# Low halves of the layer weights: from GpSimd to VectorE in the mixing part of a layer

## The chip, the cores and the metric

The kernel runs on one core of one Trainium2 chip. The metric is the device time of one execution in microseconds (us); less is better. TensorE (PE), VectorE (DVE), ScalarE (ACT), GpSimd (POOL) and SyncE (SP, which issues the DMAs) each run their own list of instructions in order and meet through semaphores.

## The reference

A first block (attention, pooling, a mixture of experts, a gated projection) is followed by two equal layers of a second block. Only these two layers are touched. Cut to what is computed:

```python
for l in range(2):
    x = x + 0.5 * swiglu(rms_norm(x, ffa_norm[l]), ffa_w_in[l], ffa_w_out[l])      # feed-forward, part 1
    h = rms_norm(x, mix_norm[l])
    (c_q, c_kv, k_rope, g_q, g_k, g_v, g_b, g_a, g_z, m_qkv, gate_logits) = split_cols(h @ w_in[l], IN_SPLITS)
    o_mla = mla_branch(...)      # latent attention: up-projection, norm of each head, RoPE, causal attention
    o_gdn = gdn_branch(...)      # convolution, l2 norm, gated delta rule in chunks
    o_moba = moba_branch(...)    # norm of each head, RoPE, causal attention
    up = einsum('bsnw,nwd->bsnd', stack([o_mla, o_gdn, o_moba], axis=2), w_branch[l])
    x = x + sum(sigmoid(gates) * up, axis=2) @ w_out[l]
    x = x + 0.5 * swiglu(rms_norm(x, ffb_norm[l]), ffb_w_in[l], ffb_w_out[l])      # feed-forward, part 2
```

256 rows, width 1024, everything in float32.

## The kernel before, in words

**Split weights.** A float32 product is made of three faster ones (`mm3`, L502): each operand is held as a high part in the type fp32r and a low part, which is the rest. Activations are split where they are made. Weights come from memory in float32 and are split on the chip. They stream in steps (`STEPS`, L36), each of two halves of 2048 words a partition (`HALVES`), each half of two pieces of 1024 words (some smaller). A piece passes four engines:

- SP loads it into one of four buffers `raw` (L1676), once the piece that lay there four pieces ago has its low part (semaphore `weights_split`).
- ACT writes the high part into `w_hi` (`hi_act`, L483), one of three slots of a half each. Before the first piece of a half it waits until PE has used the half that lay in the slot, three halves back (`half_read`).
- POOL subtracts and writes the low part into `w_lo` (`lo_pool`, L489).
- PE waits for the low part of a half and multiplies (`weights`, L493, and L504 to L506).

ACT's copies stand between its other work, where `Splits.ahead(step)` (L430) is called: it puts out all pieces of the halves up to three beyond the last of the step named. POOL has nothing else to do in a layer.

**Order in a layer.** Feed-forward part 1, the mixing part (`MIX_STEPS`, L33), feed-forward part 2. In the mixing part PE runs: `mla` (the latents), gates 0, up-projection, gates 1 and 2, latent attention; `moba` 0 to 2, gates 3 and 4, branch 0, the second attention; `gdn` 0 to 2, `z`, gates 5, the delta rule (`gdn_pe`, L749), branches 2 and 1, output projection. VectorE works on what PE needs next: the head norms (L644 to L650) and RoPE (L662 to L667), on which the transposes of an attention (L309) wait; the convolution (L913, L915) and the l2 norm (L926 to L934), on which the delta rule waits; the sum of the branches (L1838 to L1847), on which the output projection waits. PSUM has eight banks, and PE claims a bank only when its reader has freed it (`claim`).

Of the diff's functions `gdn_dve` (from L885) and the blocks of `layer_body` (from L1668) hold most of the places that the texts name.

Of the kernel before, what the change touches and what calls it, by code (L numbers as in the profile page):

```python
# [423 lines left out]
class Splits:  # L424
# [5 lines left out]
    def ahead(self, step):  # L430

        upto = min(last_half_of(step) + SPLIT_SLOTS + 1, len(HALVES))
# [52 lines left out]

def lo_pool(k, pool, i):
    for n, at in pieces(i):
        pool.wait_ge(k.sem("weights_hi"), n + 1)
        k.nc.gpsimd.tensor_tensor(k.w[1][i % SPLIT_SLOTS][:, at], k.raw[n % RAW_SLOTS][:, 0:at.stop - at.start],  # L489
                                  k.w[0][i % SPLIT_SLOTS][:, at], ALU.subtract).then_inc(k.sem("weights_split"), 1)  # L490


def weights(k, pe, step, shape):  # L493

    own = [i for i, h in enumerate(HALVES) if h[0] == STEP[step]]
    for h, i in enumerate(own):
        pe.wait_ge(k.sem("weights_split"), 2 * i + 2)
        words = HALVES[i][2]
        yield h, h == len(own) - 1, [k.w[j][i % SPLIT_SLOTS][:, 0:words].rearrange("p (c n) -> p c n", n=shape) for j in range(2)]
# [47 lines left out]
def norm2_dve(k, dve, link, n, gain, power):  # L547
    nc, st = k.nc, k.s(STATS, SCRATCH - STATS)
    V_ = nc.vector
    dve.wait_ge(k.sem("ss_ready"), 2 * (n + 1))  # L550
    rstd_dve(k, dve, link, st[:, 0:2], 1.0 / D, power)
    for t in range(NT):
        V_.tensor_scalar(k.h[:, t, :], k.x[:, t, :], st[:, t:t + 1], None, ALU.mult).then_inc(k.sem("h_ready"), 1)
    for half in range(2):
# [63 lines left out]
def ffn_dve(k, dve, n):  # L618
    nc = k.nc
    silu, prod = k.s(SILU_TMP, 2, 512), k.s(SILU_TMP + 1024, 2, 512)  # L620
    for kind, u in FFN_STEPS:
        if kind == "out":
            continue
        b, free = k.filled(dve, ("up", n, u))
# [260 lines left out]
def gdn_dve(k, dve, link):  # L885
# [21 lines left out]
    for i in range(3):  # L907
        k.evacuated(dve, ("raw", i, 0), ("raw", i, 1))
        for j in range(4):
# [35 lines left out]
    link(V_.tensor_copy(G.XT[:, :].rearrange("p t h n -> p (t h) n"), bc(k.c("ident").unsqueeze(1), [P, 8, P])))  # L945
    branch_dve(k, dve, 2)
# [710 lines left out]
def layer_body(k, dram, layer):  # L1657
# [9 lines left out]
    with nc.Block() as block:  # L1667
        @block.sync  # L1668
        def _(sp):
            sp.dma_start(k.lvec[:, :], dram["lvec"][bass.ds(layer, 1)].rearrange("o p n -> (o p) n")).then_inc(k.sem("lvec_loaded"), 16)  # L1670
            for i, (step, at, _words) in enumerate(HALVES):
                for n, part_at in pieces(i):
                    if n >= RAW_SLOTS:
                        sp.wait_ge(k.sem("weights_split"), n - RAW_SLOTS + 1)
# [117 lines left out]
        def _(dve):  # L1792
# [3 lines left out]
            norm2_dve(k, dve, link, 0, k.lv("g_ffa"), 0)  # L1796
            ffn_dve(k, dve, 0)
            norm2_dve(k, dve, link, 1, k.lv("g_mix"), 1)
            k.evacuated(dve, ("mla", 0), ("mla", 1))
# [10 lines left out]
            ins.then_inc(k.sem("c_ready"), 1)  # L1810
            gain = k.lv("c_norm")
# [12 lines left out]
            dve.wait_ge(k.sem("k_rope"), 2)  # L1824
            k.evacuated(dve, *[(x, t, i) for t in range(NT) for x in ("q", "kv") for i in range(2)])
            head_norm_dve(k, dve, link, mla.qk, k.s(QKT, 32, MLA_D), MLA_D, (k.lv("q_norm"), k.lv("k_norm")), 3)
            rope_dve(k, dve, link, mla.qk, QKT, 64, 16, k.c("cos16"), k.c("sin16"), k.sem("qk_ready"))
            mask = lambda t, pair: bc(causal[:, (1 - t) * P:2 * P].unsqueeze(1), [P, 2, (t + 1) * P])
            attn_dve(k, dve, link, mla, MLA_D ** -0.5, mask)
            k.evacuated(dve, *[("moba", i, t) for i in range(3) for t in range(NT)])  # L1830
            head_norm_dve(k, dve, link, moba.qk, k.s(QKT, 32, MOBA_D), MOBA_D, (k.lv("moba_q"), k.lv("moba_k")), 4)
            rope_dve(k, dve, link, moba.qk, QKT, 0, 32, k.c("cos32"), k.c("sin32"), k.sem("qk_ready"))
            branch_dve(k, dve, 0)
            attn_dve(k, dve, link, moba, MOBA_D ** -0.5, mask)
            gdn_dve(k, dve, link)

            branches = gatesT.rearrange("p (n c) s -> p n c s", n=3)
            link(V_.tensor_tensor(comb, branches[:, 0], branches[:, 2], ALU.add))  # L1838
            branch_dve(k, dve, 1)
# [8 lines left out]
            for v in range(2):  # L1848
                for t in range(NT):
# [4 lines left out]
            ffn_dve(k, dve, 1)  # L1854
# [178 lines left out]
```

## Time and profile before

| | us |
|---|---|
| Median of 3 runs (2852.99 to 2853.11) | 2853.03 |
| Span of the profiled execution, first to last instruction | 2852.2 |
| Layer 0: first matmul of the layer to that of layer 1 | 1172.65 to 2016.25, 843.6 |
| of it the mixing part, about | 436 |
| PE busy over the span | 2534.9 (89%) |
| DVE, ACT, POOL busy | 973.9, 888.3, 1027.5 |

The profile gives the profiled execution's span; what lies around it is the difference to the median, 0.8 us. A busy PE is not at its peak: its clock has two levels, 2.4 GHz (granted clock 1.0) and 1.2 GHz (0.5). Layer 1 repeats layer 0 to within 0.5 us, so the texts speak of layer 0 and count twice. Times in the rows are us from the start of the span.

### The profile page before, as it was taken

To read this page: it belongs to the slowest core of one execution; us is meant where nothing else is said; L and a number is where in the kernel's file an instruction comes from. 1 tells how busy PE (TensorE), PEld (TensorE's weight loads), DVE (VectorE), ACT (ScalarE), POOL (GpSimd) and SP (SyncE) were. 2 spreads that over 40 slices of the span, in tenths; PEclk is the share of its full clock that TensorE was granted. 3 is DMA by queue.
4 is the path that set the end of the run, shared out by engine and by line. 5 is a ranking of instruction groups with operands and counts; after the bars stand their busy time and mean duration, and the time that the engine had idled before them with its cause. 6 is when DMAs were issued, how large, how long until landed. Compare 5 with 4: busy or idle time off the path is not lost. (4 is left out here: it accounts for less than half of the span.)

```text
span 2852.2 us, 37927 instructions
## 1 busy us (share of the span) xinstructions
PE 2534.9 (89%) x15142; PEld 1826.0 (64%) x15142; DVE 973.9 (34%) x1514; ACT 888.3 (31%) x1266; POOL 1027.5 (36%) x428
## 2 busy tenths in 40 slices
PE   8889999999999998799778976899799777986899
PEld 3544443434434343599767866899799767875898
DVE  0322121212222121311465775221211557774221
ACT  1311212111111211444344531343444444431342
POOL 0000000000000000488548521688688546522686
PEclk9889999999999999899889997999899888997999
DMA  8249999999999995455325320354455324311453
GB/s 333 97 180 428 429 428 428 429 428 429 427 430 427 430 428 243 134 185 185 133 68 170 103 75 30 132 185 157 161 186 185 123 86 136 119 60 40 153 187 138
DMA packets 94236, 650.66 MB, mean 228 GB/s; under 512 B 10448, under 2 KB 12416, under 8 KB 68128
## 3 DMA queue, kind: packets, MB, share of 16 engines
q1 hardware_dynamic: 94112, 648.94, 58.8%
q8 instruction: 86, 1.41, 0.2%
q14 instruction: 38, 0.31, 0.0%
HBM read 647.84 MB, written 1.06 MB: 228 GB/s over the span
## 5 line engine op out<-in xcount | busy, mean ns | idle before, releaser
L489 POOL TENSOR_TENSOR w_lo<-raw,w_hi 128x1024 fp32r<-128x1024 f32 (+3 forms) x424 | 1027.3, 2446 | 1807.5 <-ACT w_hi L483 1807.5
L1319 PE MATMUL bank<-ring,scratch 128*64 128x512 f32 x3072 | 686.1, 596 | 27.2 <-DMA ring<-in_expert_units 25.4
L483 ACT CAST w_hi<-raw 128x1024 fp32r<-128x1024 f32 (+3 forms) x424 | 419.8, 1038 | 672.0 <-PE bank L506 659.6
L504 PE MATMUL bank<-hT_hi,w_hi 128*128 128x256 f32 x1984 | 566.1, 285 | 18.6 <-ACT scratch L1762 9.5
L505 PE MATMUL bank<-hT_lo,w_hi 128*128 128x256 f32 x1984 | 565.0, 285 | 0.0
L506 PE MATMUL bank<-hT_hi,w_lo 128*128 128x256 f32 x1984 | 564.9, 285 | 0.0
L1319 PEld LDWEIGHTS bank<-ring,scratch 128*64 128x64 f32 x3072 | 209.7, 137 | 455.0 <-issue 386.7
L504 PEld LDWEIGHTS bank<-hT_hi,w_hi 128*128 128x128 f32 x1984 | 384.8, 194 | 21.6 <-issue 10.5
L505 PEld LDWEIGHTS bank<-hT_lo,w_hi 128*128 128x128 f32 x1984 | 384.8, 194 | 0.8
L506 PEld LDWEIGHTS bank<-hT_hi,w_lo 128*128 128x128 f32 x1984 | 384.5, 194 | 0.0
L1487 DVE TENSOR_TENSOR scratch<-bank,scratch 128x512 f32<-128x512 f32 x64 | 44.3, 692 | 605.0 <-PE bank L1333 601.1
L626 DVE TENSOR_TENSOR scratch<-scratch,bank 128x512 f32<-128x512 f32 x44 | 30.3, 688 | 539.2 <-ACT scratch L612 539.2
L504 PE MATMUL bank<-w_hi,act_hi 128*128 128x512 f32 (+1 forms) x376 | 147.2, 392 | 6.9 <-ACT scratch L1027 6.9
L505 PE MATMUL bank<-w_lo,act_hi 128*128 128x512 f32 (+1 forms) x376 | 147.1, 391 | 0.0
L506 PE MATMUL bank<-w_hi,act_lo 128*128 128x512 f32 (+1 forms) x376 | 146.7, 390 | 0.0
L1305 PEld LDWEIGHTS bank<-scratch,h_rows 128*128 128x128 f32 x1056 | 124.9, 194 | 27.5 <-issue 27.5
L1305 PE MATMUL bank<-scratch,h_rows 128*128 128x128 f32 x1056 | 133.8, 281 | 0.0
L745 PE MATMUL bank<-scratch 128*128 128x128 f32 x816 | 106.0, 293 | 26.2 <-DVE scratch L986 7.3
L745 PEld LDWEIGHTS bank<-scratch 128*128 128x128 f32 x816 | 102.4, 206 | 32.0 <-issue 18.0
L1388 ACT COPY scratch<-bank 128x512 f32<-128x512 f32 x64 | 37.5, 586 | 265.9 <-PE bank L1319 265.9
L1390 ACT ACTIVATE scratch<-scratch 128x256 f32<-128x256 f32 x64 | 26.7, 417 | 276.2 <-DVE scratch L1490 276.2
L629 DVE TENSOR_TENSOR act_lo<-scratch,act_hi 128x512 fp32r<-128x512 f32 x44 | 102.3, 2324 | 30.2 <-ACT act_hi L615 30.2
(263 smaller groups left out, 2832.8 us busy)
## 6 DMA issues: line engine op xcount, KB each, us to landing
ring<-in_expert_units SPq DMA_DIRECT2D x192, 2048.0 KB, 20.5
raw<-in_layer_units SPq DMA_DIRECT2D x408, 512.0 KB, 4.7
ring<-in_first_units SPq DMA_DIRECT2D x6, 2048.0 KB, 23.9
ring<-in_ple_units SPq DMA_DIRECT2D x2, 2048.0 KB, 9.9
raw<-in_layer_units SPq DMA_DIRECT2D x8, 424.0 KB, 3.4
raw<-in_layer_units SPq DMA_DIRECT2D x4, 384.0 KB, 3.2
const<-in_const SPq DMA_DIRECT2D x1, 1184.0 KB, 7.3
x_res<-in_x SPq DMA_DIRECT2D x1, 1024.0 KB, 4.9
```

The source lines that it names most:

```text
L483: k.nc.scalar.copy(k.w[0][i % SPLIT_SLOTS][:, at], k.raw[n % RAW_SLOTS][:, 0:at.stop - at.start]).then_inc(k.sem("weights_hi"), 1)
L489: k.nc.gpsimd.tensor_tensor(k.w[1][i % SPLIT_SLOTS][:, at], k.raw[n % RAW_SLOTS][:, 0:at.stop - at.start], k.w[0][i % SPLIT_SLOTS][:, at], ...
L504: nc.tensor.matmul(out, lhsT[0], rhs[0], start=start, stop=False)
L505: nc.tensor.matmul(out, lhsT[0], rhs[1], start=False, stop=False)
L506: return nc.tensor.matmul(out, lhsT[1], rhs[0], start=False, stop=stop)
L626: nc.vector.tensor_tensor(prod[:, u % 2, :], silu[:, u % 2, :], b[:, :], ALU.mult).then_inc(free, 1)
L629: nc.vector.tensor_tensor(lo, prod[:, u % 2, :], hi, ALU.subtract).then_inc(k.sem("act_lo"), 1)
L745: last = nc.tensor.matmul(b[:, h * P:(h + 1) * P], lhsT[:, h, :], rhs[:, h, :], start=True, stop=True)
L1305: last = nc.tensor.matmul(b[:, j * P:(j + 1) * P], k.h[:, t, c * P:(c + 1) * P], sel[:, t, :], start=(t == 0), stop=(t == 1))
L1319: last = nc.tensor.matmul(b[g * SL:(g + 1) * SL, :], lhsT[:, c, :], w[:, c, g, :], start=start and c == 0, stop=stop and c == 3)
L1388: nc.scalar.copy(rows[:, half, :], b[:, :]).then_inc(free, 1)
L1487: V_.tensor_tensor(both, b[:, :].rearrange("p (a n) -> p a n", n=SL), bc(wide_bias, [P, 8, SL]), ALU.add)\
```

## The change

The low parts of the 80 pieces of the mixing part are now computed by VectorE (`lo_dve`), those of the feed-forward parts still by GpSimd (132 pieces a layer). The semaphore `weights_split` is replaced by two, and `split_done` says for a piece which one and which count. In `gdn_dve` and in VectorE's block of `layer_body` calls of `splits.ahead` (and of the new `to`) are put between its other work, at about the places where ScalarE has them. ScalarE's and TensorE's instructions keep their order.

```diff
+FIRST_MIX = sum(1 for h in HALVES if STEPS[h[0]][0] == "ffn0")
+LAST_MIX = sum(1 for h in HALVES if STEPS[h[0]][0] != "ffn1")
+def split_done(k, n):
+    i = n // 2
+    if FIRST_MIX <= i < LAST_MIX:
+        return k.sem("mix_weights_split"), n - 2 * FIRST_MIX + 1
+    return k.sem("ffn_weights_split"), n + 1 if i < FIRST_MIX else n + 1 - 2 * (LAST_MIX - FIRST_MIX)
...
+def lo_dve(k, dve, i):
+    if not FIRST_MIX <= i < LAST_MIX:
+        return
+    for n, at in pieces(i):
+        dve.wait_ge(k.sem("weights_hi"), n + 1)
+        k.nc.vector.tensor_tensor(k.w[1][i % SPLIT_SLOTS][:, at], k.raw[n % RAW_SLOTS][:, 0:at.stop - at.start],
+                                  k.w[0][i % SPLIT_SLOTS][:, at], ALU.subtract).then_inc(k.sem("mix_weights_split"), 1)
...
-        pe.wait_ge(k.sem("weights_split"), 2 * i + 2)
+        pe.wait_ge(*split_done(k, 2 * i + 1))
...
-                        sp.wait_ge(k.sem("weights_split"), n - RAW_SLOTS + 1)
+                        sp.wait_ge(*split_done(k, n - RAW_SLOTS))
...
+            splits.ahead(STEP["gates", 0])
             gain = k.lv("c_norm")
...
+            splits.ahead(STEP["up_proj", 0])
             k.evacuated(dve, *[(x, t, i) for t in range(NT) for x in ("q", "kv") for i in range(2)])
             head_norm_dve(k, dve, link, mla.qk, k.s(QKT, 32, MLA_D), MLA_D, (k.lv("q_norm"), k.lv("k_norm")), 3)
+            splits.ahead(STEP["gates", 1])
             rope_dve(k, dve, link, mla.qk, QKT, 64, 16, k.c("cos16"), k.c("sin16"), k.sem("qk_ready"))
...
+            splits.ahead(STEP["gates", 2])
             attn_dve(k, dve, link, mla, MLA_D ** -0.5, mask)
+            for i in range(3):
+                splits.ahead(STEP["moba", i])
             k.evacuated(dve, *[("moba", i, t) for i in range(3) for t in range(NT)])
             head_norm_dve(k, dve, link, moba.qk, k.s(QKT, 32, MOBA_D), MOBA_D, (k.lv("moba_q"), k.lv("moba_k")), 4)
+            splits.ahead(STEP["gates", 3])
             rope_dve(k, dve, link, moba.qk, QKT, 0, 32, k.c("cos32"), k.c("sin32"), k.sem("qk_ready"))
+            splits.ahead(STEP["gates", 4])
+            splits.ahead(STEP["branch", 0])
             branch_dve(k, dve, 0)
...
             branches = gatesT.rearrange("p (n c) s -> p n c s", n=3)
             link(V_.tensor_tensor(comb, branches[:, 0], branches[:, 2], ALU.add))
+            splits.ahead(STEP["branch", 1])
             branch_dve(k, dve, 1)
...
         def _(pool):
             for i in range(len(HALVES)):
-                lo_pool(k, pool, i)
+                if not FIRST_MIX <= i < LAST_MIX:
+                    lo_pool(k, pool, i)
```

VectorE, head norm and RoPE of the latent attention, before (L647 and L650 end the norm, L662 to L667 are RoPE, whose first half is shown):

```order
L647 TENSOR_TENSOR scratch<-scratch 128x3072
L650 TENSOR_TENSOR scratch<-scratch,lvec 128x1536 x2
L662 TENSOR_TENSOR scratch<-scratch,const 128x256
L663 TENSOR_TENSOR scratch<-scratch,const 128x256
L664 TENSOR_TENSOR scratch<-scratch,const 128x256
```

And after the change (the lines have moved: L676, L679 and L691 are L647, L650 and L662 of before; L514 is the new subtraction):

```order
L676 TENSOR_TENSOR scratch<-scratch 128x3072
L679 TENSOR_TENSOR scratch<-scratch,lvec 128x1536 x2
L514 TENSOR_TENSOR w_lo<-raw,w_hi 128x1024 x4
L691 TENSOR_TENSOR scratch<-scratch,const 128x256
L692 TENSOR_TENSOR scratch<-scratch,const 128x256
L693 TENSOR_TENSOR scratch<-scratch,const 128x256
```

Four pieces stand between the norm and RoPE now; in the second attention four stand at the same place.

VectorE, end of the convolution and l2 norm of the delta rule, before (L915 convolution, L923 squares, L926 to L934 l2 norm):

```order
L915 SCALAR_TENSOR_TENSOR scratch<-scratch,lvec 128x256 x12
L923 TENSOR_TENSOR scratch<-scratch 128x1024 x2
L926 TENSOR_SCALAR scratch<-bank 128x512 x4
L930 RECIPROCAL scratch<-scratch 128x512 x4
L933 SCALAR_TENSOR_TENSOR scratch<-scratch 128x1024
```

And after the change:

```order
L945 SCALAR_TENSOR_TENSOR scratch<-scratch,lvec 128x256 x12
L514 TENSOR_TENSOR w_lo<-raw,w_hi 128x1024 x4
L954 TENSOR_TENSOR scratch<-scratch 128x1024 x2
L957 TENSOR_SCALAR scratch<-bank 128x512 x4
L514 TENSOR_TENSOR w_lo<-raw,w_hi 128x1024 x4
L962 RECIPROCAL scratch<-scratch 128x512 x4
L965 SCALAR_TENSOR_TENSOR scratch<-scratch 128x1024
```

Four pieces stand ahead of the squares and four ahead of the reciprocals.

## Rows read from the trace of the kernel before

**Rows 1.** The page: the span.

```profile
span 2852.2 us, 37927 instructions
```

**Rows 2.** Windows: feed-forward 1, mixing; us, busy PE, PEld, DVE, ACT, POOL, PEclk, DMA share, GB/s.

```profile
1172.00:1367.00 195.00, 191.07 (x1335) 180.54 (x1336) 42.80 (x47) 82.88 (x93) 165.04 (x70) 0.98 0.56 187
1367.00:1803.00 436.00, 342.72 (x2269) 312.15 (x2268) 265.85 (x324) 168.56 (x271) 200.06 (x81) 0.87 0.29 95
```

**Rows 3.** Waits of PE, both layers: waiting line, releaser, total us, times, longest.

```profile
PE bank L309 <- DVE scratch L667: 52.8, 4, 14.1
PE bank L504 <- DVE hT_lo L1847: 17.6, 2, 8.8
PE bank L755 <- DVE scratch L923: 10.8, 2, 5.4
```

**Rows 4.** The page's groups: busy us, mean ns; idle before, releaser.

```profile
L489 POOL TENSOR_TENSOR w_lo<-raw,w_hi 128x1024 fp32r<-128x1024 f32 (+3 forms) x424 | 1027.3, 2446 | 1807.5 <-ACT w_hi L483 1807.5
L483 ACT CAST w_hi<-raw 128x1024 fp32r<-128x1024 f32 (+3 forms) x424 | 419.8, 1038 | 672.0 <-PE bank L506 659.6
```

**Rows 5.** Groups of DVE by form.

```profile
L629 DVE TENSOR_TENSOR act_lo<-scratch,act_hi 128x512 fp32r<-128x512 f32 x44 | 102.3, 2324 | 30.2 <-ACT act_hi L615 30.2
...
L626 DVE TENSOR_TENSOR scratch<-scratch,bank 128x512 f32<-128x512 f32 x44 | 30.3, 688 | 539.2 <-ACT scratch L612 539.2
...
L923 DVE TENSOR_TENSOR scratch<-scratch 128x1024 f32<-128x1024 f32 x4 | 4.7, 1220 | 0.0
```

**Rows 6.** Timeline of DVE, norm to RoPE: start, duration, operation, [idle before].

```profile
1371.66 1.68 DVE L205 TENSOR_SCALAR scratch<-scratch 128x2 f32<-128x2 f32 x1 [3.42 <-ACT h_rows L233]
...
1402.80 0.56 DVE L1815 TENSOR_TENSOR act_hi<-bank,lvec 128x384 fp32r<-128x384 f32 x1 [3.46 <-PE bank L1695]
...
1426.27 3.35 DVE L645 TENSOR_REDUCE scratch<-scratch 128x32 f32<-128x3072 f32 x1
...
1437.42 5.53 DVE L647 TENSOR_TENSOR scratch<-scratch 128x3072 f32<-128x3072 f32 x1 [5.37 <-ACT scratch L212]
1442.99 7.66 DVE L650 TENSOR_TENSOR scratch<-scratch,lvec 128x1536 f32<-128x1536 f32 x2
...
1458.91 0.42 DVE L667 TENSOR_TENSOR scratch<-scratch 128x256 f32<-128x256 f32 x1
```

**Rows 7.** Timeline of ACT around gates 0 and gates 2.

```profile
1402.47 1.99 ACT L483 CAST w_hi<-raw 128x1024 fp32r<-128x1024 f32 x2 [4.19 <-PE bank L506]
...
1447.27 1.08 ACT L1027 ACTIVATE scratch<-bank 128x512 f32<-128x512 f32 x2
```

**Rows 8.** Timeline of PE: both attentions, l2 norm, after branch 2.

```profile
1459.39 0.88 PE L309 MATMUL bank<-const,scratch 128*96 128x128 f32 x3 [14.06 <-DVE scratch L667]
...
1564.64 5.33 PE L309 MATMUL bank<-const,scratch 128*64 128x128 f32 x32 [12.36 <-DVE scratch L667]
...
1658.64 1.55 PE L755 MATMUL bank<-scratch,const 128*128 128x512 f32 x3 [1.79 <-ACT scratch L1027]
...
1682.87 1.16 PE L780 MATMUL bank<-const,scratch 128*128 128x128 f32 x8 [1.67 <-DVE scratch L1612]
```

**Rows 9.** Windows after a wait of PE (4.75 us before 1420.03); columns as in rows 2.

```profile
1420.00:1424.40 4.40, 4.37 (x20) 4.40 (x21) 3.24 (x1) 1.03 (x4) 3.01 (x2) 0.50 0.62 212
1424.70:1445.30 20.60, 20.60 (x172) 20.43 (x171) 15.09 (x6) 9.75 (x11) 14.01 (x6) 1.00 0.38 124
```

**Rows 10.** Timeline of DVE, second attention: end of the norm, RoPE.

```profile
1532.86 4.47 DVE L647 TENSOR_TENSOR scratch<-scratch 128x2048 f32<-128x2048 f32 x1 [4.33 <-ACT scratch L212]
1537.37 6.67 DVE L650 TENSOR_TENSOR scratch<-scratch,lvec 128x1024 f32<-128x1024 f32 x2
1544.07 2.78 DVE L662 TENSOR_TENSOR scratch<-scratch,const 128x512 f32<-128x512 f32 x1
```

**Rows 11.** Timeline of DVE, delta rule: reciprocals of the l2 norm.

```profile
1661.27 12.98 DVE L930 RECIPROCAL scratch<-scratch 128x512 f32<-128x512 f32 x4
```

**Rows 12.** Timeline of ACT, after the convolution: high parts behind L859.

```profile
1652.81 3.87 ACT L483 CAST w_hi<-raw 128x1024 fp32r<-128x1024 f32 x4
```

More of the change, by code:

```diff
@@ L430, in ahead, with to @@
     def ahead(self, step):
-        upto = min(last_half_of(step) + SPLIT_SLOTS + 1, len(HALVES))
+        self.to(last_half_of(step) + SPLIT_SLOTS + 1)
+    def to(self, end):
+        upto = min(end, len(HALVES))
         for i in range(self.done, upto):
@@ L489, in lo_pool @@
         k.nc.gpsimd.tensor_tensor(k.w[1][i % SPLIT_SLOTS][:, at], k.raw[n % RAW_SLOTS][:, 0:at.stop - at.start],
-                                  k.w[0][i % SPLIT_SLOTS][:, at], ALU.subtract).then_inc(k.sem("weights_split"), 1)
+                                  k.w[0][i % SPLIT_SLOTS][:, at], ALU.subtract).then_inc(k.sem("ffn_weights_split"), 1)
+def lo_dve(k, dve, i):
[5 more added lines that the diff above has]
+                                  k.w[0][i % SPLIT_SLOTS][:, at], ALU.subtract).then_inc(k.sem("mix_weights_split"), 1)
 def weights(k, pe, step, shape):
@@ L542, in rows3_pe, with norm2_dve @@
             last.then_inc(k.sem("half_used"), 1)
-def norm2_dve(k, dve, link, n, gain, power):
+def norm2_dve(k, dve, link, n, gain, power, between=lambda: None):
     nc, st = k.nc, k.s(STATS, SCRATCH - STATS)
@@ L553, in norm2_dve @@
         V_.tensor_scalar(k.h[:, t, :], k.x[:, t, :], st[:, t:t + 1], None, ALU.mult).then_inc(k.sem("h_ready"), 1)
+    between()
     for half in range(2):
@@ L615, in ffn_act, with ffn_dve @@
         k.nc.scalar.copy(k.act2[0][:, at:at + 2, :].rearrange("p c n -> p (c n)"), prod[:, u % 2, :]).then_inc(k.sem("act_hi"), 1)
-def ffn_dve(k, dve, n):
+def ffn_dve(k, dve, n, splits):
     nc = k.nc
@@ L622, in ffn_dve @@
         if kind == "out":
+            if u < FFN_OUT_UNITS - 1:
+                splits.ahead(STEP[f"ffn{n}", kind, u])
             continue
+        splits.ahead(STEP[f"ffn{n}", kind, u])
         b, free = k.filled(dve, ("up", n, u))
@@ L882, in gdn_act, with gdn_dve @@
         nc.scalar.copy(k.act2[0][:, 4:8, t * P:(t + 1) * P], part(b, 4, P)).then_inc(k.sem("go_hi"), 1)
-def gdn_dve(k, dve, link):
+def gdn_dve(k, dve, link, splits):
     nc, G = k.nc, Gdn(k)
@@ L907, in gdn_dve @@
     for i in range(3):
+        splits.ahead(STEP["gdn", i])
         k.evacuated(dve, ("raw", i, 0), ("raw", i, 1))
@@ L919, in gdn_dve @@
                 ins.then_inc(k.sem("conv_ready"), 1)
+    splits.ahead(STEP["z", 0])
     for i in range(2):
@@ L926, in gdn_dve @@
         V_.tensor_scalar(G.sq[:, 2 * b4:2 * b4 + 2, :], part(b, 2, S), EPS, None, ALU.add).then_inc(free, 1)
+    splits.ahead(STEP["gates", 5])
     for b4 in range(4):
@@ L945, in gdn_dve @@
     link(V_.tensor_copy(G.XT[:, :].rearrange("p t h n -> p (t h) n"), bc(k.c("ident").unsqueeze(1), [P, 8, P])))
+    splits.ahead(STEP["branch", 2])
     branch_dve(k, dve, 2)
@@ L1795, in _ @@
             dve.wait_ge(k.sem("lvec_loaded"), 16)
-            norm2_dve(k, dve, link, 0, k.lv("g_ffa"), 0)
-            ffn_dve(k, dve, 0)
+            splits = Splits(k, dve, lo_dve)
+            norm2_dve(k, dve, link, 0, k.lv("g_ffa"), 0, lambda: splits.to(1))
+            splits.to(SPLIT_SLOTS)
+            ffn_dve(k, dve, 0, splits)
             norm2_dve(k, dve, link, 1, k.lv("g_mix"), 1)
+            splits.ahead(STEP["ffn0", "out", 5])
+            splits.ahead(STEP["mla", 0])
             k.evacuated(dve, ("mla", 0), ("mla", 1))
@@ L1848, in _ @@
             for v in range(2):
+                if v == 0:
+                    splits.ahead(STEP["wout", v])
                 for t in range(NT):
@@ L1853, in _ @@
             norm2_dve(k, dve, link, 2, k.lv("g_ffb"), 6)
-            ffn_dve(k, dve, 1)
+            splits.ahead(STEP["wout", 1])
+            ffn_dve(k, dve, 1, splits)
         @block.gpsimd
```

2 lines of the change are left out of this document (1 added, 1 removed).

## The prediction

> **What bounds the kernel now.** I read the windows first, then PE's waits, then the timelines of VectorE, ScalarE and PE around the longest waits. In the feed-forward window PE is busy 191 of 195 us; in the mixing window 343 of 436 [rows 2]. What can be won lies in the mixing window. PE's waits name no POOL instruction: the low part is never late. A piece costs POOL 2.45 us [rows 4], so a half 4.9, while PE needs 5.76 for one (48 matmuls at 20.60/172 = 0.12 us [rows 9]). PE waits for VectorE: 52.8 us for the end of RoPE, 17.6 for the sum of the branches, 10.8 for the end of the convolution [rows 3].
>
> POOL does matter in another way. VectorE's L626 (one input in PSUM) takes 0.69 us, and L629, as long but with both inputs in SBUF, 2.32 [rows 5]. In the second attention the 512-long L662 takes 2.78, against the 0.69 of L626 [rows 5, 10]: it waits some 2.1 us, most of one POOL instruction. The 1024-long L650 takes 3.33 each, against 1.22 for L923 [rows 5, 10]. So VectorE and POOL block each other when both read SBUF, and just in the head norms, on which PE waits.
>
> The Trainium skill has this in "SBUF — State Buffer", Who interferes with whom: VectorE with two SBUF inputs and GpSimd take turns at a shared port, and the loser waits for the whole instruction. By the rows the wait is about 2.1 of 2.45 us. By the whole-instruction rule each blocked VectorE instruction would gain some 0.3 us more than I count, about 2 us a layer; I go by the rows.
>
> **The change, step by step, for layer 0, in the clock of before.** It moves 80 pieces a layer to VectorE. Durations: 1.22 us (L923 [rows 5]) for 1024 long; lengths 3072 and 1536 without POOL are 3.35 (L645 [rows 6]) and, between 1.22 and 3.35, 1.75; a short RoPE instruction 0.38 from start to start (0.42 with overlap [rows 6]), a long one 0.61 to 0.69. 80 x 1.22 = 98 us on an engine busy 266 of 436 [rows 2]: it does not become the bound by its sum. The question is what each group of pieces stands in front of, and when PE gets its halves: it holds at most three that are ready.
>
> 1. *Norm before mixing.* L205 takes 1.68 us for two elements [rows 6], a wait for POOL. VectorE makes the last pieces before it. Bounds 0 to -1.68; I take -1.5.
> 2. *Up-projection.* VectorE starts L1815 at 1402.80. Now the last two pieces of `ahead(gates 0)` stand ahead, whose high parts ACT writes from 1402.47 to 1404.46 [rows 6, 7]: second low part at 1405.7, and L1815 is 2.9 late, of which 0.7 was cover, since PE waits for ACT's sigmoid too. +2.2. Position +0.7.
> 3. *First attention.* PE waited 14.06 us until 1459.39 [rows 8], so gates 2 ended at 1445.3 and the half before it at 1439.6. After the change PE stops at 1440.3, since the last half of gates 2 is split only behind L650. L647 starts when ACT has the root (1437.42 [rows 6]) + 0.7, then 3.35 + 2 x 1.75: 1445.0. Two pieces: 1447.4. PE stops 7.1 us, then 5.76: 1453.2. It needs a bank that ACT frees: 2.6 us, as before (L1027 at 1447.27 [rows 7] + 0.6, against 1445.3): 1455.8. RoPE is ready earlier (1445.0 + 4 x 1.2 + 12 x 0.38 = 1454.4). L309 starts at 1455.8 for 1459.39: position -3.6, term -4.3.
> 4. *Second attention.* The same. PE's wait was 12.36 until 1564.64 [rows 8], so its halves ended at 1535.0, 1540.8, 1546.5, 1552.3. It stops at 1535.0; L650 ends at 1532.86 + 2.3 + 2.4 = 1537.6 (2.3: two of 1.22, less one fixed cost), and two pieces later, 1540.0, it goes on: a stop of 5. Three halves: 1557.3; the last is split behind RoPE (1542.4 + 12 x 0.61 + 2.4 = 1552.1), some 0.8 late: 1558.1, for 1564.64, -6.5. But banks 4 to 7 are freed by L1612, now behind eight pieces, whose high parts follow PE's last halves: I take +2.4 (bounds 0 and 8 x 1.22 = 9.8). Term -4.1.
> 5. *Convolution.* Without POOL its 48 instructions end before PE is through with gates 5, with 12 pieces among them. PE's wait of 5.4 (half of 10.8 [rows 3]) goes. The third L755 waits for ACT's sigmoid at 1658.64 [rows 8], behind L483 that started only at 1652.81 [rows 12], when the convolution was done; this moves forward by as much as PE allows. I take -4.6 (bounds 0 and -5.4).
> 6. *l2 norm.* Four pieces stand ahead of the reciprocals (12.98 us, no wait ahead [rows 11]), on which the delta rule waits. 4 x 1.15: +4.6, no cover.
> 7. *Branch 2.* Four more ahead of L1612, on which L780 waits [rows 8]: +4.8, of which up to 1.7 is PE's slack there; +3.1.
> 8. *Output projection.* Four pieces ahead of branch 1's evacuation, mostly under PE's matmuls. +1.0 (bounds 0 and 4.9).
>
> Sum: -1.5 + 2.2 - 4.3 - 4.1 - 4.6 + 4.6 + 3.1 + 1.0 = -3.6 a layer. The feed-forward parts are unchanged.
>
> 9. *TensorE's clock.* After a wait of 4.75 us PE did 20 matmuls in 4.4 us at granted clock 0.50 (1.2 GHz), where 2.4 GHz does 20 x 0.12 = 2.4 [rows 9]: a stop costs 2.0 more. Before, the two long waits were followed by transposes; now two new stops are followed by dense matmuls. Bounds 0 and +4.0 a layer, and below nothing too, since elsewhere waits vanish; I take one, +2.2.
>
> Net -1.4 a layer, -2.8 for two. The profiled execution spans 2852.2, 0.8 below the median [rows 1]: 2852.2 - 2.8 + 0.8 = **2850.2 us**.
>
> "TensorE: Matmul & The Clock Gate", HAM oscillation, in the Trainium skill says that a matmul stream cut up by waits is throttled again at each, which speaks against this change. By it both stops cost, and the sum is near nothing; a result of its own only with more stops, below.
>
> **Rivals.** 0.2% is 5.7 us, about what a measurement of this kernel tells from no change.
>
> *Forecast: losses and gains cancel* (chance 0.40). Within 2847 to 2859. For it: two groups of terms of about 13 us each a layer, on the same engine.
>
> *The port pays more* (0.35), 2840 to 2847. The steps won are full, and the pieces of steps 6 to 8 find cover: if 7 and 8 cost half and the clock nothing, it is -3.6 - 2.0 = -5.6 a layer, 2842. For it: the gains are read from rows, PE's wait of 12.36 us [rows 8] could be nearly all won. Against: step 6 stands bare.
>
> *Slower, by the clock* (0.25), 2859 to 2870. The two long waits become many short ones, PE runs at 1.2 GHz behind each. It decides from the third stop on that is followed by dense matmuls: with both stops of steps 3 and 4, one more in the moba and branch halves and one at branch 1, 4 x 2.0 = 8 for the 2.2 that I took: -3.6 + 8 = +4.4 a layer, 2862. For it: granted clock 0.87 in the mixing window with ten waits over 2 us. Against: the long waits' own restart goes.
>
> *VectorE's waits for high parts hold back the critical work*, part of that chance: a subtraction waits for ACT, ACT for PE, and what is queued behind it on VectorE waits with it. The worst place is before L1612 (step 4); at its bound of 9.8 it gives +7.4 a layer more, 2865.
>
> *It doesn't do what it says* (below 0.02): POOL would still run in the mixing part.
>
> Range for 8 of 10: 2839 to 2864. Faster by over 0.2% 0.35, within 0.40, slower 0.25.
>
> **What would show it.** POOL idle in the mixing window, VectorE near 266 + 98 - 50 = 314 busy. Right: L650's counterpart at 1.22 and 1.75; PE waits before a half of gates 2 (some 7 us) and of gates 4 (some 5), both with the new subtraction as releaser; PE's wait for RoPE gone or under 3; the wait before L755 gone; the delta rule's start 7 to 8 us later against the end of gates 5. Wrong: long waits of PE for RoPE that stay (then the port was not the cause), stops for low parts elsewhere, or a granted clock in the mixing window under 0.85.

## The result, and the profile after

The changed kernel takes 2866.44 us (four executions, 2859.28 to 2872.11), the kernel before 2853.07 beside it: ratio 1.0044, 95% interval 1.0029 to 1.0058. It is slower by 13 us; 2850.2 were predicted, in a range up to 2864. Fifteen executions in three sets have the median 2868.7; two lie at 2859, the rest between 2865 and 2872. The first profiled one, from which the rows here are, is the fastest of them (2859.28). One execution of one experiment (`after_between`) took 6918.6 us where its five others took 2832 to 2842, and is left out of its ratio.

Its windows for the feed-forward and the mixing part of layer 0, with the columns of [rows 2]:

```profile
1171.60:1367.00 195.40, 191.12 (x1329) 180.66 (x1330) 45.61 (x49) 83.64 (x95) 157.19 (x66) 0.97 0.58 188
1367.00:1810.00 443.00, 355.07 (x2277) 322.52 (x2275) 280.04 (x403) 171.35 (x273) 10.11 (x5) 0.87 0.30 95
```

GpSimd has gone from the mixing part: its 10 us in this window are pieces of the feed-forward part. VectorE is busy 280 us of it; the pieces in the window cost 88, and 74 of that came back from its other instructions (265.9 + 87.8 - 280.0). The prediction had 50 coming back and 314 busy. The 1024-long subtraction, by VectorE's groups by form:

```profile
L514 DVE TENSOR_TENSOR w_lo<-raw,w_hi 128x1024 fp32r<-128x1024 f32 x144 | 169.3, 1221 | 126.8 <-ACT w_hi L487 126.4
```

TensorE's waits over both layers (waiting line, releaser, total, times, longest), to be held against [rows 3]:

```profile
PE bank L529 <- DVE w_lo L514: 24.7, 4, 7.2
...
PE bank L529 <- DVE hT_lo L1894: 19.2, 2, 9.6
...
PE bank L809 <- DVE scratch L1645: 12.6, 2, 6.4
...
PE bank L774 <- DVE scratch L966: 11.0, 2, 5.6
...
PE bank L309 <- DVE scratch L1645: 6.4, 2, 3.7
PE bank L309 <- ACT scratch L1060: 6.4, 2, 3.4
```

The 52.8 us for the end of RoPE and the 10.8 for the end of the convolution are gone. In their place stand stops for a low part (7.24 and 5.11 us in each layer), and for what VectorE does behind its pieces: L809 behind the evacuation of branch 2 (L1645), L774 behind the l2 norm (L966), the transposes L309. The wait for the sum of the branches stays and grows (19.2 for 17.6).

VectorE in the first attention, where [rows 6] are its rows of before (start, duration, operation, idle before):

```profile
1428.71 0.18 DVE L205 TENSOR_SCALAR scratch<-scratch 128x32 f32<-128x32 f32 x1
...
1437.60 3.36 DVE L676 TENSOR_TENSOR scratch<-scratch 128x3072 f32<-128x3072 f32 x1 [8.32 <-ACT scratch L212]
1440.99 3.56 DVE L679 TENSOR_TENSOR scratch<-scratch,lvec 128x1536 f32<-128x1536 f32 x2
1444.58 4.63 DVE L514 TENSOR_TENSOR w_lo<-raw,w_hi 128x1024 fp32r<-128x1024 f32 x4
1449.13 0.42 DVE L691 TENSOR_TENSOR scratch<-scratch,const 128x256 f32<-128x256 f32 x1
```

The norm's product takes 3.36 us for 5.53, the two gain products 3.56 for 7.66. But ScalarE's root comes 3 us later after its reciprocal than before (8.32 us of idle for 5.37), and four pieces of 1.15 stand ahead of RoPE.

Cut at TensorE's first instruction of each stage, a layer divides as follows. "Before" is the mean of its two layers, "after" the mean over three profiled executions (`after`, `after_again` and `after_third`: 2859, 2870 and 2866 us), all in us; the second layer's last feed-forward part is taken to TensorE's last instruction; "port free" and "pieces short" are two experiments told below.

| stretch, by TensorE | before | after | predicted change | measured | port free | pieces short |
|---|---|---|---|---|---|---|
| norm before mixing to the first attention | 83.8 | 84.7 | -2.1 | +0.9 | 72.9 | 79.8 |
| to the second attention | 105.3 | 99.5 | -6.5 | -5.8 | 93.4 | 98.3 |
| second attention | 25.6 | 28.1 | +2.4 | +2.5 | 24.6 | 25.1 |
| convolution, to the end of the l2 sums | 70.2 | 64.1 | -4.6 | -6.1 | 64.4 | 63.9 |
| l2 norm, to the KK products | 17.3 | 21.9 | +4.6 | +4.6 | 17.4 | 17.7 |
| to the transposes of v (branch 2) | 5.1 | 10.0 | +3.1 | +4.9 | 5.1 | 8.4 |
| delta rule | 71.2 | 72.1 | 0 | +0.9 | 71.7 | 71.3 |
| branch 1, output projection | 56.7 | 58.9 | +1.0 | +2.2 | 53.0 | 56.7 |
| both feed-forward parts | 401.1 | 401.8 | -1.5 | +0.7 | 400.6 | 401.1 |

Step 1 of the prediction (-1.5) shortens TensorE's wait ahead of the norm's first product, so it lies in the last row, and steps 2 and 3 make the -2.1 of the first. Predicted -3.6, and +2.2 for the clock: -1.4. Measured +4.7 in this mean of profiles, 9.4 for two layers. The three spans are 10.9 us longer than before; the other 1.5 lie ahead of layer 0, where no instruction was changed.

### The profile page after: what moved, and what is told of

Its sections match the earlier page's. It is cut to its first block and busy times, and to the rows that moved or that the text cites. A ratio compares the mean times of both kernels' runs of the same rounds, so it can differ in the third digit from the quotient of the medians.

```text
span 2857.4 us, 37933 instructions
## 1 busy us (share of the span) xinstructions
PE 2552.6 (89%) x15142; PEld 1841.7 (64%) x15142; DVE 1006.0 (35%) x1674; ACT 890.4 (31%) x1266; POOL 628.7 (22%) x268
## 5 line engine op out<-in xcount | busy, mean ns | idle before, releaser
L505 POOL TENSOR_TENSOR w_lo<-raw,w_hi 128x1024 fp32r<-128x1024 f32 x264 | 628.5, 2402 | 2211.5 <-ACT w_hi L487 2211.5
L1352 PE MATMUL bank<-ring,scratch 128*64 128x512 f32 x3072 | 685.9, 596 | 26.3 <-DMA ring<-in_expert_units 24.5
L514 DVE TENSOR_TENSOR w_lo<-raw,w_hi 128x1024 fp32r<-128x1024 f32 (+3 forms) x160 | 183.6, 1191 | 137.6 <-ACT w_hi L487 137.2
L774 PE MATMUL bank<-scratch 128*128 128x128 f32 x816 | 110.4, 301 | 29.3 <-DVE scratch L966 11.0
L774 PEld LDWEIGHTS bank<-scratch 128*128 128x128 f32 x816 | 106.1, 213 | 34.5 <-issue 15.8
```

What stands on the lines that cost most here:

```text
L514: k.nc.vector.tensor_tensor(k.w[1][i % SPLIT_SLOTS][:, at], k.raw[n % RAW_SLOTS][:, 0:at.stop - at.start], k.w[0][i % SPLIT_SLOTS][:, at], ...
L774: last = nc.tensor.matmul(b[:, h * P:(h + 1) * P], lhsT[:, h, :], rhs[:, h, :], start=True, stop=True)
L1352: last = nc.tensor.matmul(b[g * SL:(g + 1) * SL, :], lhsT[:, c, :], w[:, c, g, :], start=start and c == 0, stop=stop and c == 3)
```

## Experiments

All were timed in five rounds beside the kernel before. Its medians there were 2854.3 to 2855.7, a few executions up to 2861; so small differences are read from the ratios.

**The change again, its two stops filled, the stops alone.** Three kernels on one chip. The first has no edit:

> The changed kernel once more. The kernel before spread over 0.7 us in four executions, the changed one over 12.8 us (2859.3 to 2872.1), its span in step with TensorE's mean granted clock (0.940 at 2857.4, 0.932 at 2870.3). Theory C (the clock): the new stops of TensorE make the pattern of half-speed stretches differ between executions; then this run spreads by 5 us or more again, median 2862 to 2870, and the slower executions are those with the lower clock. Theory W (VectorE's waits and its added work): the cost is fixed by the order of instructions, so the times lie within 1.5 us of each other, at one value between 2859 and 2870.

2868.94 us, ratio 1.0035 (1.0021 to 1.0049). One execution in six at 2859.4 with granted clock 0.938, five at 2868.7 to 2869.6 with 0.933 or 0.934: theory C's signs are there (over 5 us between executions, the slower ones at the lower clock), but as two values and not as a spread. The rest of the fifteen executions lie between and above them.

```diff
+            if step in FILL:      # gates 2: 52 products, gates 4: 38, between the two halves
+                fill(k, pe, step) # matmul(b[:, 0:S], k.hT2[0][:, 0, 0:P], k.hT2[0][:, 0, :])
```

> The changed kernel, with products that nobody reads (52 of 128x256 before the second half of gates 2, 38 before that of gates 4) in TensorE's two new stops of 7.2 and 5.1 us. At full speed they take 52 x 0.12 = 6.2 us and 38 x 0.12 = 4.6 us, so they fit into the stops. Theory C: the clock keeps its pattern of before, the time falls to 2850 to 2856 and the spread to under 2 us. Theory W: the stops' length and everything on VectorE are as they were, so the time stays at 2859 to 2870, or rises where the fillers run at half speed and overfill the stops.

2867.63 us, ratio 1.0036 (1.0024 to 1.0049). Nothing gained, and the profile says why. The filled stop kept the granted clock at 1.00: the half behind it in gates 2 took 6.0 us, where in `after_again` it took 8.2. But TensorE then waited 5.1 us for ScalarE's evacuation ahead of the transposes, instead of 2.7 to 2.8, and they started no earlier (85.7 and 85.6 us after the norm's first product, for 85.6 and 85.5). What the clock costs behind this stop is hidden under ScalarE. Behind the stop in gates 4 TensorE took 18.0 us to the second attention's transposes instead of 18.6 and 18.7, but the stop ended 1.8 us later, counted from the first attention; the cause of that stays open.

```diff
+        if h == 1 and step in STOPS:      # {("gates", 2): 21, ("gates", 4): 40}
+            pe.wait_ge(k.dve_step, STOPS[step])
```

> The kernel before, unchanged but for two waits of TensorE: before the second half of gates 2 for the first gain product of the first attention's norm, before that of gates 4 for the same product of the second attention. By the trace of the kernel before these make stops of about 7.3 and 5.5 us, and what TensorE still has to do in either place then ends ahead of the rotary step that it waits for anyway (1451.3 against 1459.4, 1557.8 against 1564.6), so no time is lost but by the clock. Theory C: slower than before by 5 to 15 us, and a spread of over 3 us. Theory W: within 1 us of before, spread under 1 us.

2851.98 us against 2855.55, ratio 0.9990 (0.9981 to 0.9998). The stop was there:

```profile
1447.16 0.55 PE L509 MATMUL bank<-hT_hi,w_hi 128*128 128x256 f32 x1 [7.34 <-DVE scratch L655]
```

and no time was lost. That does not settle theory C. The clock did fall behind the stop: 24 of the half's 48 products at granted clock 0.50, and 8.24 us for the half instead of 5.76 (first the part at 0.50, then the whole half; columns as in [rows 2]):

```profile
1447.16:1452.30 5.14, 5.14 (x24) 5.14 (x25) 5.11 (x5) 0.00 (x0) 2.08 (x1) 0.50 0.52 168
1447.16:1455.40 8.24, 8.24 (x48) 8.04 (x48) 8.07 (x13) 0.00 (x0) 2.08 (x1) 0.69 0.34 111
```

RoPE ended at 1455.37 and the transposes started only at 1458.07, so these 2.5 us did delay them; they are outweighed, since in the kernel before they started at 1459.39. For the run gains elsewhere: while TensorE stands, halves are not used up and GpSimd has nothing to split, so all RoPE products of the first attention run at 0.42 us (the first two took 2.44 and 2.56 before), and all but the last of the second at 0.69. The stretches to the two attentions are 2.9 and 4.9 us shorter than before, enough to hide a loss. The spread does not decide either: the eleven executions lie between 2848.7 and 2857.9, more than theory W allows, but those of the kernel before beside them lie between 2852.8 and 2861.4.

**The pieces into VectorE's wait for the root.**

```diff
     k.nc.vector.reciprocal(v, v).then_inc(k.sem("inverse_variance"), 1)
+    between()       # in the attentions' norms: splits.ahead(STEP["gates", 1]), (["gates", 3])
     dve.wait_ge(k.sem("rstd_ready"), n + 1)
-            splits.ahead(STEP["gates", 1])      # stood between norm and RoPE; so did gates 3
```

> The changed kernel with the four pieces that stand between an attention's head norm and its rotary step moved into that norm, behind its reciprocal, where VectorE waited 8.3 and 6.5 us for ScalarE's root. That takes both stops of TensorE away and 4.6 us from the path of either attention. Theory C: 2 x 2 x 4.6 = 18 us less from the path at most, some of it lost where ScalarE's own work comes last, and the clock's loss gone too: 2842 to 2852, spread under 3 us. Theory W: only the path's part is gained, from 2866 to 2848 to 2858, and the spread says nothing. If the root is itself held up (ScalarE issues high parts ahead of it that wait for raw pieces, and those for low parts), the gain is smaller still.

2835.98 us (five executions from 2832.2 to 2842.0, clock 0.940 to 0.946), ratio 0.9930 (0.9918 to 0.9943): below both expectations. The stretch to the first attention is 73.8 and 75.4 us in the two layers, 9 to 11 less than after the change, more than the four pieces' 4.6. TensorE's stop for a low part is gone too, and so is its wait for ScalarE: the transposes now wait 3.61 us for RoPE. That low parts which come early free their raw buffers early fits this, but no run separates it.

**Where the 80 pieces cost.** `pool_late` sets `LAST_MIX = 66`, so that the last seven halves are GpSimd's. `three_moves` is that, the edit above, and `splits.ahead(STEP["branch", 0])` behind `branch_dve(k, dve, 0)`. The other two cut the subtractions of the mixing part:

```diff
+        at = slice(at.start, at.start + 8)      # before_no_mix: GpSimd's; after_no_mix: VectorE's
```

> The changed kernel, but the low parts of the last seven halves of the mixing part (second half of branch 2, branch 1, the output projection) are GpSimd's again; VectorE keeps those up to gates 5 and the first half of branch 2. Theory P (place: pieces issued where VectorE's own work is on the path): the stretches behind the convolution go back to what they took before, 21.9 to 17.3 us (l2 norm to the first KK product), 9.95 to 5.1 us (KK to the transposes of v), 58.8 to 56.7 us (end of the delta rule to the next norm), 11.5 us a layer or 23 in all: 2869 becomes 2846, if the clock's share stays. Theory C (only the clock's pattern is to blame): the spread of values 2859 to 2870 stays, since no stop ahead of dense products is taken away.

2845.40 us, ratio 0.9957 (0.9943 to 0.9970): 2846 was expected. In the profile, l2 norm to KK 17.4, KK to the transposes of v 5.1, branch 1 to the next norm 57.2 us. VectorE in the l2 norm after the change, and in `pool_late`:

```profile
1652.00 4.62 DVE L514 TENSOR_TENSOR w_lo<-raw,w_hi 128x1024 fp32r<-128x1024 f32 x4
1656.54 12.98 DVE L962 RECIPROCAL scratch<-scratch 128x512 f32<-128x512 f32 x4
```

```profile
1655.35 0.69 DVE L957 TENSOR_SCALAR scratch<-bank 128x512 f32<-128x512 f32 x1 [0.86 <-PE bank L784]
1655.96 12.98 DVE L962 RECIPROCAL scratch<-scratch 128x512 f32<-128x512 f32 x4
```

> Three edits together: the pieces of either attention behind the norm's reciprocal (2835.98 with that alone), those named for branch 0 behind the products with branch 0's gates instead of ahead of them, and the last seven halves on GpSimd. Theory P: another 11.5 us a layer for the last and 3.5 to 4.4 us a layer for the middle one (TensorE's stop in the transposes for the second attention's keys, 3.9 and 3.0 us in one execution, 4.4 and 4.1 in another): 2836 - 31 = 2805, with up to 5 us a layer less where the scores no longer fall into a half-speed stretch. Theory C: 2830 to 2842.

2812.15 us, ratio 0.9847 (0.9833 to 0.9860): 7 us above the expectation. A stop of TensorE had moved, from the second attention's transposes to just behind them (5.1 and 5.5 us, for ScalarE's copies).

> The kernel before, with GpSimd's subtractions for the mixing part cut from 1024 columns to 8, so that most of those low parts are left out. It measures what GpSimd's work there costs VectorE. From the forms of VectorE with and without it beside them (norm product 5.53 to 3.36, two gain products 7.66 to 3.56, two rotary products 5.0 to 0.8, the small scale 1.8: 12.3 us in the first attention; in the second 21 us, of which TensorE's own work to the end of branch 0 lets 10 through; convolution 5.6): 28 us a layer, 2853 to 2797. If the neighbour's work costs VectorE nothing on the path: 2850 to 2856.

2787.18 us, ratio 0.9753 (0.9740 to 0.9767). GpSimd's work in the mixing part costs the kernel before 68 us, more than the 56 expected. In "SBUF — State Buffer", Who interferes with whom, the Trainium skill says that an instruction of VectorE with two SBUF inputs contends with a GpSimd instruction that reads SBUF: the long RoPE products of the second attention, 2.78 us in [rows 10], take 0.69 here. The 68 us hold all that GpSimd's work costs, also through the clock (granted 0.949 for 0.942) and the buffers; they are not the waits at the port alone.

> The changed kernel, with VectorE's subtractions cut from 1024 columns to 8, so that most low parts of the mixing part are left out; the waits for high parts and the places stay. What falls away is VectorE's own time in the pieces, 1.15 us each, 80 a layer. Theory P: most of what stands on the path is this time (4 pieces at the l2 norm, 4 at branch 2, 4 in either attention ahead of the rotary step, 4 ahead of branch 0's products): 20 x 1.1 = 22 us a layer, 2869 to 2825, and it lies above the kernel before without that work by what the waits for high parts cost. Theory C: 2855 to 2865. If the waits for high parts were the dear part, it stays near 2869.

2827.83 us, ratio 0.9902 (0.9887 to 0.9918), 2825 expected. So, by the ratios against 2855.6: the change takes 70 us off (GpSimd's work gone, 1 - 0.9753), adds 43 for the places of the pieces and the waits for high parts (0.9902 - 0.9753), and 38 for VectorE's own time in them (1.0035 - 0.9902). The last two columns of the table say where: ahead of both attentions, of the transposes of v and in the row of branch 1 it is mostly the waits ("pieces short" less "port free"), at the l2 norm the pieces' own time.

**The second attention.** In an execution of `after_again` at 2869.6 us, ScalarE and then VectorE around the start of its transposes:

```profile
2408.43 1.05 ACT L487 CAST w_hi<-raw 128x1024 fp32r<-128x1024 f32 x1 [3.74 <-DMA raw<-in_layer_units]
2410.80 1.05 ACT L487 CAST w_hi<-raw 128x1024 fp32r<-128x1024 f32 x1 [1.32 <-DMA raw<-in_layer_units]
2413.35 1.04 ACT L487 CAST w_hi<-raw 128x1024 fp32r<-128x1024 f32 x1 [1.50 <-DMA raw<-in_layer_units]
2414.57 1.04 ACT L487 CAST w_hi<-raw 128x1024 fp32r<-128x1024 f32 x1 [0.17 <-DMA raw<-in_layer_units]
2415.52 2.01 ACT L355 COPY scratch<-bank 64x512 f32<-64x512 f32 x4
```

```profile
2411.88 1.22 DVE L514 TENSOR_TENSOR w_lo<-raw,w_hi 128x1024 fp32r<-128x1024 f32 x1 [1.15 <-ACT w_hi L487]
2414.43 2.44 DVE L514 TENSOR_TENSOR w_lo<-raw,w_hi 128x1024 fp32r<-128x1024 f32 x2 [1.32 <-ACT w_hi L487]
2416.79 2.47 DVE L1645 TENSOR_TENSOR scratch<-bank,scratch 128x512 f32<-128x512 f32 x4
```

A circle: VectorE waits for ScalarE's high part, ScalarE for raw weights, these for a buffer that VectorE's low part frees. Branch 0's evacuation (L1645) and ScalarE's copies (L355) stand behind it. TensorE there, and its clock (columns as in [rows 2]):

```profile
2412.07 1.58 PE L309 MATMUL bank<-const,scratch 128*64 128x128 f32 x13
2417.52 3.62 PE L309 MATMUL bank<-const,scratch 128*64 128x128 f32 x16 [3.87 <-DVE scratch L1645]
2422.01 10.58 PE L318 MATMUL bank<-scratch 64*128 64x128 f32 x32 [0.86 <-ACT scratch L355]
```

```profile
2411.76:2417.75 5.99, 2.12 (x20) 1.82 (x18) 4.55 (x5) 4.09 (x7) 0.00 (x0) 0.90 0.85 305
2417.75:2421.75 4.00, 3.39 (x16) 2.47 (x14) 1.51 (x3) 2.30 (x4) 0.00 (x0) 0.50 0.67 214
2421.75:2432.25 10.50, 10.24 (x32) 8.57 (x32) 7.87 (x18) 6.92 (x26) 0.00 (x0) 0.50 0.00 1
```

```diff
-            splits.ahead(STEP["branch", 0])     # ScalarE; on VectorE likewise
             attn_act(k, act, moba)
+            splits.ahead(STEP["branch", 0])
```

> The changed kernel (2869), with both parts of the two halves that are named for branch 0 (high on ScalarE, low on VectorE; the second half of the convolution's first unit and the first of its second) issued behind the second attention instead of ahead of branch 0's products and of the attention. Theory P: TensorE's stop in the transposes for the keys (4.4 and 4.1 us) goes, and ScalarE copies the transposed keys without first waiting for raw weights; from the start of those transposes to the end of the attention 30.8 us become 25 to 26.5, 9 to 12 us in both layers: 2857 to 2860. Theory C's part in it: 4.9 of the 30.8 us are the score products at half speed; if the stop brings that on, they come at full speed now (9.9 us become 5.1) and it is 2857; if the half-speed stretch comes anyway, it is 2860 to 2864.

2852.37 us, ratio 0.9991 (0.9982 to 1.0000): this one move takes the whole loss back, 12.6 us by the ratios, against 9 to 12 expected. TensorE in the same place:

```profile
2401.45 3.66 PE L309 MATMUL bank<-const,scratch 128*64 128x128 f32 x32
2406.30 5.48 PE L318 MATMUL bank<-scratch 64*128 64x128 f32 x32 [1.19 <-ACT scratch L355]
```

No stop, and the scores take 5.48 us for 10.58. The second attention takes 24.2 and 23.8 us in the two layers, for 30.9 and 30.8.

> Three edits of before together (pieces of either attention behind the norm's reciprocal, the last seven halves on GpSimd) with the one of behind_attention in place of the simpler one. In the run of three moves TensorE stood 5.4 us between transposes and scores, behind ScalarE, which waited for raw weights. Theory P: that stop goes, 4 to 5 us a layer: 2812 becomes 2802 to 2804. If it was hidden: 2810 to 2814.

2805.24 us, ratio 0.9828 (0.9814 to 0.9841), the best version: 49 us under the kernel before, granted clock 0.949.

```diff
-            splits.ahead(STEP["gates", 1])      # ScalarE
+            splits.to(43)
             rstd_act(k, act, k.s(STATS + 128, 2 * NT * H), 3)
+            splits.ahead(STEP["gates", 1])
```

> four_moves, and in the first attention ScalarE takes the root ahead of the high part of the first unit of the second attention's projection (which waits for the end of gates 1), with its low part on VectorE behind the rotary step. The root came 7.2 us after its reciprocal, and TensorE waited 3.6 us for the rotary step at the transposes: 3 us a layer less, 6 in all, if the pieces behind the rotary step are ready before the scores: 2797; if they hold the first score step back, as much is lost there: 2803.

2811.43 us, ratio 0.9848 (0.9835 to 0.9862), a miss. RoPE ends 68.0 and 70.9 us into the mixing part, 6 to 9 earlier than in `four_moves`, but the transposes start at 78.4 and 80.6, 2 to 4 later. TensorE waits there, and ScalarE shows for what:

```profile
1453.77 5.84 PE L310 MATMUL bank<-const,scratch 128*96 128x128 f32 x32 [8.23 <-ACT scratch L1061]
```

```profile
1448.83 1.04 ACT L488 CAST w_hi<-raw 128x1024 fp32r<-128x1024 f32 x1 [7.02 <-DMA raw<-in_layer_units]
1452.08 1.04 ACT L488 CAST w_hi<-raw 128x1024 fp32r<-128x1024 f32 x1 [2.20 <-DMA raw<-in_layer_units]
1453.03 1.08 ACT L1061 ACTIVATE scratch<-bank 128x512 f32<-128x512 f32 x2
```

The low part that I moved behind RoPE freed its raw buffers later, and the evacuation of gates 2 (L1061) stood behind the high parts that waited for them.

**Stop or clock.** The second attention's stop filled with work, and the same stop put back into `behind_attention`:

```diff
-                for j in range(4):
+                for j in [0] * (34 if (n, q, t, half) == (1, 0, 1, 1) else 0) + [0, 1, 2, 3]:
```

> The changed kernel (2869), with 34 repeated transposes of 0.107 us, 3.6 us together, into the bank that the last four transposes of the queries fill, so that TensorE works through its stop of 4.1 to 4.4 us ahead of the keys' transposes in the second attention, and nothing else moves (ScalarE copies from that bank only after this time anyway). It tells the two parts of behind_attention's 16.5 us apart. If the stop itself brings on the half-speed stretch that the score products fell into, these come at full speed (5.1 us instead of 9.9) and the time is 2858 to 2862. If the stop costs only its length and what waits behind it, the time stays at 2867 to 2871.

2857.65 us (2854.1 to 2868.3), ratio 1.0009 (1.0000 to 1.0018): the median is what the first part of the expectation had. But the profiled execution is the slowest (2868.3), and in it the scores took 9.3 and 8.4 us with the stop filled.

> The changed kernel a third time, now on the same chip as keys_filled_2. Its two executions profiled so far stood at 2859.3 and 2869.6; six more of after_again at 2859.4 and 2868.7 to 2869.5. Expected: 2862 to 2870 again. If the chip and not the filled stop made the 11 us between after_again and keys_filled, this one too comes at 2856 to 2860.

2867.83 us (2866.0 to 2869.8), ratio 1.0039 (1.0026 to 1.0052).

> keys_filled once more, beside the changed kernel itself. If the filled stop is what counts: 2854 to 2860 in most executions, 8 to 12 us under after_third. If it was the chip: no difference of over 2 us between the two.

2862.27 us (2852.7 to 2872.3), ratio 1.0015 (1.0004 to 1.0027): 5.6 us under `after_third` on the same chip, less than expected, and with the widest spread of all. In its profile the keys' transposes run at granted clock 1.00, but in the window of the scores it is 0.57, and they took 8.6 us in both layers. So working through the stop shortens most executions, but the half-speed stretch can come without a stop.

```diff
+            for _ in range(3):      # VectorE, behind branch_dve(k, dve, 0); TensorE waits for "held"
+                link(V_.tensor_tensor(k.h[:, 1, :], k.h[:, 0, :], k.h[:, 0, :], ALU.subtract))
+            V_.tensor_tensor(k.h[:, 1, :], k.h[:, 0, :], k.h[:, 0, :], ALU.subtract).then_inc(k.sem("held"), 1)
```

> behind_attention (2852.4), with a stop of about 4 us put back into TensorE's transposes for the keys by another way: VectorE, idle there, does four subtractions of 1024 columns that nobody reads (1.15 us each), and TensorE waits for the last. If a stop costs its length only, it is 4 us a layer in each of two layers: 2859 to 2861. If a stop there also brings the score products to half speed (9.9 us instead of 5.1), it is 2866 to 2870.

2865.16 us, ratio 1.0031 (1.0020 to 1.0043): 11.4 us above `behind_attention` by the ratios, between the two expectations. The stops are just under 4 us in each layer, 8 in both. The picture of `after_again` is back, with the clock at 0.50 from the second half of the transposes:

```profile
2410.98 3.62 PE L311 MATMUL bank<-const,scratch 128*64 128x128 f32 x16 [3.94 <-DVE h_rows L1883]
2415.47 10.58 PE L320 MATMUL bank<-scratch 64*128 64x128 f32 x32 [0.86 <-ACT scratch L357]
```

The scores lose 5.1 us, of which the value transposes behind them, which otherwise wait for VectorE, give back 3.0 (from their first to their last 6.6 us for 9.6). So in this profile a stop costs its length and some 2 us (11.4 us in two layers against 8 of stops, by ratios that are each uncertain by about 3 us). "TensorE: Matmul & The Clock Gate", HAM oscillation, in the Trainium skill says that a stream cut by waits is throttled again at each: the trace agrees for this stop and for the one ahead of the half of gates 2, where the cost was hidden.

The length of a stop does not decide what follows. In the profiles of `after_between` and `pool_late`, the same place in layer 1:

```profile
2381.87 3.62 PE L310 MATMUL bank<-const,scratch 128*64 128x128 f32 x16 [5.09 <-DVE scratch L1646]
2386.36 5.47 PE L319 MATMUL bank<-scratch 64*128 64x128 f32 x32 [0.87 <-ACT scratch L356]
```

```profile
2406.45 2.86 PE L309 MATMUL bank<-const,scratch 128*64 128x128 f32 x16 [2.97 <-DVE scratch L1645]
2410.18 10.58 PE L318 MATMUL bank<-scratch 64*128 64x128 f32 x32 [0.87 <-ACT scratch L355]
```

After 5.09 us the transposes ran at 0.50, but the clock was back at 1.00 for the scores; after 2.97 us the scores ran wholly at 0.50. In `before_stops`, with no stop in the transposes and 2.63 us between them and the scores, these took 10.5 and 10.6 us.

## Why the prediction was wrong

*Right: where the neighbour's work costs, and where the change gives it back.* GpSimd's work beside VectorE was the cause of the long RoPE waits (`before_no_mix`); L205, L679 and RoPE came at the predicted durations. Steps 5 and 6 measured -6.1 and +4.6 for -4.6 and +4.6; step 5 went beyond its bound of -5.4. The stops of steps 3 and 4 were 7.24 and 5.11 us for 7.1 and 5, step 4's term -3.3 in the mean for -4.1. That its +2.4 for the second attention meets the mean of +2.5 is luck: by profile and layer it was +0.5 to +5.2.

*The step that failed most is step 3.* It gave the half behind the stop 5.76 us, and ScalarE 2.6 us more to free the bank, "as before". ScalarE's evacuation of gates 2 stood behind four high parts that waited for raw weights, in the profile of the changed kernel:

```profile
1450.27 1.04 ACT L487 CAST w_hi<-raw 128x1024 fp32r<-128x1024 f32 x1 [10.30 <-DMA raw<-in_layer_units]
...
1457.56 0.59 ACT L1060 ACTIVATE scratch<-bank 128x512 f32<-128x512 f32 x1
```

L309 started at 1458.29 for the 1455.8 predicted, in the fastest execution. In the mean of three, steps 2 and 3 together are +0.9 for -2.1. Of these 3.0 us some 1.0 is the reference: layer 0, from which the prediction was worked out, has 84.8 us before, the mean of the layers 83.8. In the three profiles the half behind the stop took 7.9 to 8.2 us for 5.76, at granted clock 0.50 in part, and ScalarE freed the bank 2.7 to 3.4 us later for 2.6; TensorE came to the stop some 0.9 earlier than predicted. Filling the stop took the clock's part away and gained nothing, because ScalarE's high parts still waited for raw weights: the wait that ends last here is that one, which the step did not have.

*Step 1 was mis-sized:* L205 went from 1.68 to 0.17 us, but TensorE's wait ahead of the norm fell only from 7.11 to 6.47, 0.6 us for 1.5. The root comes 1.15 us after the reciprocal instead of 0.27, since ScalarE's table load (1.28 us) ends only then.

*Steps 7 and 8 were mis-sized:* +4.9 for +3.1 and +2.2 for +1.0. `pool_late` brings back 4.9 and 1.7 of them. At branch 2, 3.3 of the 4.9 us were still there with the pieces cut short: mostly waits for high parts, which the step did not count, and not the pieces' own 4.6.

*Step 9 had only part of the clock.* I charged +2.2 for the two stops ahead of gates. The clock fell behind both; behind the first it is hidden (above). Behind the second the three halves to the transposes took 18.6 to 20.1 us, and 18.0 with the stop filled: 0.7 to 2.1 us a layer. What I left out is the second attention, which step 4 booked as +2.4 us of delay: there TensorE stood 2.4 to 4.1 us in the transposes, and the scores took 5.5 to 10.6 us. The rival "slower, by the clock" named a third stop as the point from which it decides and 2862 as its time; the rival of the waits for high parts named this place, at most 9.8 us. The outcome has something of both: removing the circle there takes back 6.3 us a layer. The clock alone I can't price closer than 5.6 us (`keys_filled_2`) to 11 (`keys_filled` against `after_again`, on another chip; 7.4 by the ratios), both with wide spreads.

Not settled: why most executions of the changed kernel are at 2869 and some at 2859, with the same instructions. The stretches at granted clock 0.50 lie differently in them. Of the 10.3 us between the spans of `after` and `after_again` 6.9 lie in the second attention; `after_third` is 6.7 us longer than `after` with a second attention as short as 26.3 and 26.5 us, and loses ahead of the first attention, in the delta rule, in branch 1 and in the feed-forward parts instead. What brings a stretch on in one place and not in another stays open.

## What to carry to other kernels

When a helper's work moves to an engine that has critical work, its place decides, not its sum: here 80 pieces a layer lost 6 us in one order, and 66 of them won 25 in another, by standing where the engine waited anyway, with the other 14 left to the helper. Follow the buffer circle as well: a late low part holds a raw buffer, that holds the next high part, and whatever the third engine has queued behind it. And take the upper bound, not a middle value, where pieces with waits of their own are put ahead of evacuations.

## What the hardware showed

GpSimd's work beside VectorE's cost more than I had thought: 68 us of 2855 (2.4%), for 200 us of it a layer.

One program has times from 2859 to 2872, on one chip just two, 2859 and 2869, that differ in TensorE's granted clock (0.938 and 0.934). The Trainium skill's page "TensorE: Matmul & The Clock Gate", Part 1: The HAM clock gate, says that the slow start varies between runs of one kernel and costs less than 1% of a typical one; here 10 us are 0.35%, and in the two profiles compared above most of them arise in the middle of the kernel.

A stop of 3.87 us in the second attention was followed by over 22 us at 1.2 GHz (`after_again`); one of 2.68 us at the same place, in the profile of `after_third`, was not. It is no rule of length: see `pool_late` (2.97 us, scores at half speed) and `after_between` (5.09 us, at full speed) above. The rows of `after_third`:

```profile
2414.49 2.42 PE L309 MATMUL bank<-const,scratch 128*64 128x128 f32 x16 [2.68 <-DVE scratch L1645]
2417.78 5.47 PE L318 MATMUL bank<-scratch 64*128 64x128 f32 x32 [0.86 <-ACT scratch L355]
```
